# The end of a diffusion layer on one core: token lists by matmul, experts' rows gathered and stored by index, the gate applied on the experts' results, and the last residual sum on TensorE

## The reference, cut to what matters

```python
gates: top-1 group of 4, then top-2 of its 8 experts   # 32 experts, 640 * 2 = 1280 (token, expert) pairs
y_e   = down_e(silu(gate_e(h2)) * up_e(h2))             # D -> 256 -> D, for each chosen expert e
moe   = w_top1 * y_e1 + w_top2 * y_e2
x     = LN(ALPHA * x1 + gate2 * moe) * ln2_g + ln2_b    # gate2: one row of D for context, one for latent tokens
```

## Time and profile before

| | us |
|---|---|
| median of 3 runs (2627.85 to 2636.6) | 2629.16 |
| the profiled execution, its own time | 2629.61 |
| its span, first to last instruction | 2627.7 |
| `merge` | 1720.5 to 2087 |
| `route` | 2087 to 2254 |
| `experts` | 2254 to 2565 |
| `combine` | 2565 to 2627.7 |

### The profile page before, as it was taken

The page is one execution under the profiler, slowest core; times in us unless marked ns, Lnnn a source line. Parts: engine busy times, 40 slices in busy tenths (PEclk is TensorE's granted clock), DMA queues, the critical chain, the costliest instruction groups (busy, mean ns, idle before and its releaser), DMA issues. The chain is left out here.

```text
span 2627.7 us, 27002 instructions
## 1 busy us (share of the span) xinstructions
PE 2209.9 (84%) x9907; PEld 1374.1 (52%) x9907; DVE 1068.0 (41%) x1914; ACT 508.5 (19%) x1185; POOL 373.2 (14%) x379
## 2 busy tenths in 40 slices
PE   4789889899897989898898988889999795598980
PEld 2454555455544757667585776745555444343430
DVE  3574564665743454553535545410000056111116
ACT  0121211212202323323232332300000000111111
POOL 0041051230411011010201102000000000200005
PEclk9989989899898989899998989989999896799995
DMA  7011201101001010101101010043242295399973
GB/s 267 9 49 30 65 9 40 48 8 40 32 13 55 22 34 4 32 4 34 34 2 34 4 32 14 17 144 121 73 144 72 78 306 216 141 412 420 421 322 123
DMA packets 161406, 257.71 MB, mean 98 GB/s; under 512 B 11458, under 2 KB 127257, under 8 KB 147009
## 3 DMA queue, kind: packets, MB, share of 16 engines
q1 hardware_dynamic: 150905, 221.52, 24.0%
q10 hardware_dynamic: 5512, 18.56, 1.8%
q0 software_dynamic: 4928, 16.79, 1.7%
HBM read 229.26 MB, written 27.58 MB: 98 GB/s over the span
## 5 line engine op out<-in xcount | busy, mean ns | idle before, releaser
L642 PE MATMUL bank<-hT,shared 128*128 128x512 f32 x512 | 252.9, 629 | 13.3 <-DMA negm<-in_levels_dram 8.5
L1132 PE MATMUL bank<-hT,shared 128*128 128x512 f32 x384 | 175.4, 611 | 2.9 <-ACT spadded L1271 1.6
L1974 PE MATMUL bank<-ring,xgT 128*64 128x512 f32 (+1 forms) x416 | 151.6, 634 | 25.4 <-DMA ring<-in_w_exp_up_dram 13.0
L988 DVE TENSOR_TENSOR conv<-bank,negm 128x512 f32<-128x512 f32 x144 | 82.3, 599 | 184.4 <-PE bank L655 184.4
L642 PEld LDWEIGHTS bank<-hT,shared 128*128 128x128 f32 x512 | 94.7, 201 | 96.8 <-issue 88.1
L1212 PE MATMUL bank<-shared,hT 128*128 128x512 f32 x320 | 139.9, 592 | 0.0
L655 PE MATMUL bank<-D_,MT 128*128 128x128 f32 x960 | 125.4, 279 | 0.0
L1585 DVE SCALAR_TENSOR_TENSOR prod<-gth,bank 128x512 f32<-128x512 f32 x16 | 11.0, 687 | 272.7 <-PE bank L1559 272.7
L663 PE MATMUL bank<-DT,conv 128*128 128x128 f32 x960 | 121.6, 275 | 0.0
L1132 PEld LDWEIGHTS bank<-hT,shared 128*128 128x128 f32 x384 | 73.9, 197 | 89.7 <-issue 85.9
L1194 PEld LDWEIGHTS bank<-xT,M 128*128 128x128 f32 x640 | 88.4, 218 | 54.6 <-issue 41.3
(11 more groups left out here) (394 smaller groups left out, 3557.7 us busy)
## 6 DMA issues: line engine op xcount, KB each, us to landing
shared<-in_w_in_dram SPq DMA_DIRECT2D x58, 512.0 KB, 6.3
ring<-in_w_exp_gate_dram SPq DMA_DIRECT2D x26, 1024.0 KB, 18.1
ring<-in_w_exp_up_dram SPq DMA_DIRECT2D x26, 1024.0 KB, 20.4
ring<-in_w_exp_down_dram SPq DMA_DIRECT2D x26, 1024.0 KB, 15.4
aw<-in_w_ada_dram SPq DMA_DIRECT2D x8, 2048.0 KB, 7.5
yd<-ysb ACTq DMA_DIRECT2D x22, 512.0 KB, 8.3
aw<-in_w_ada_dram SPq DMA_DIRECT2D x8, 1024.0 KB, 21.5
shared<-in_w_in_dram SPq DMA_DIRECT2D x4, 2048.0 KB, 7.6
```

What stands on the lines that cost most here:

```text
L642: last = pe.matmul(bank[a][:, :], w4[:, n, k, :], hT[:, k, SEQ:T], start=(k == 0), stop=(k == KD - 1), skip_group_check=True)
L988: TT(out=X[:, u0:u0 + n, :], in0=bank[XB[g]][:, 0:n * P].rearrange("p (u n) -> p u n", n=P), in1=m, op=ALU.mult).then_inc(s["g_Xkept"], 1)
L1132: pe.matmul(bank[a][:, :], wn(n)[:, k, :], hT[:, k, SEQ:T], start=(k == 0), stop=(k == KD - 1))
L1974: last = pe.matmul(bank[2 + slot][at, :], xgT[:, slot, k, at], wgu[w][:, k, :, :], start=(k == 0), stop=(k == KD - 1))
```

## The change

- In `route` the token list no longer goes by way of memory. DVE makes for each of the ten blocks of 128 pairs a 128x128 matrix that marks the pair's place within its row of places (`at_place`) and a 128x22 matrix with the token number plus 1 in the column of its row (`of_row`). PE adds the ten products in one bank. A place that holds 0 is empty; its index becomes NOWHERE (2 to the power 20), beyond the bounds that the indirect transfers now get. `dest` holds for each place its own number, or a number out of bounds. DVE also waits once for the zeroed `lists` tail, as `zero` now lies in `h2`.
- The first two gathers of `xg` are issued in `route`. The scatters into `lists` (which only spill blocks still need) are issued in `experts` behind the fourth gather.
- The gather of a pass and its store to `yd` are bounded by index: rows of empty places are not moved. The store is an indirect transfer on POOL.
- All of `yd` (4032 rows of 4 KB, 16.5 MB) is now zeroed in one transfer that ACT issues at the start of `merge`; before, 4864 KB of it was zeroed in `route` by SP.
- DVE chooses the gate row for each place (`gsel`) and multiplies both halves of the expert's result by it; ACT no longer copies or stores results. `g2` is loaded at the start of `experts`.
- In `combine` PE forms ALPHA * x1 plus the two weighted result rows in PSUM, with diagonal matrices `keep` (ALPHA on the diagonal) and `weigh` (the tokens' weights on it). DVE takes its statistics from the banks, ACT norms from the banks, and DVE does `back` for all five tiles.

The new tiles are made over existing ones, save a few small ones. The diff, cut to its core:

```diff
+                act.wait_ge(zero_ready, 1)
+                act.dma_start(yd.rearrange("(p b) (c n) -> p (b c) n", p=SLOT, c=4),
+                              zero[0:SLOT, :].unsqueeze(1).broadcast_to([SLOT, NPLACE // SLOT * 4, D // 4])).then_inc(yz_out, 16)
...
-                sp.dma_start(lists.rearrange("(p n) a -> p (n a)", p=SLOT), zero[0:SLOT, 0:NPLACE // SLOT]).then_inc(z_out, 16)
-                sp.dma_start(yd[NP * P:NPLACE, :].rearrange("(p b) (c n) -> p (b c) n", p=SLOT, c=4), zero[0:SLOT, :].unsqueeze(1).broadcast_to([SLOT, NMORE * 4, D // 4])).then_inc(yz_out, 16)
+                sp.dma_start(lists[NP * P:NPLACE, :].rearrange("(p n) a -> p (n a)", p=SLOT), zero[0:SLOT, 0:NMORE]).then_inc(z_out, 16)
...
-                sp.wait_ge(scattered, 16 * 2 * NT)
-                sp.dma_start(rows_[:, :], lists[0:NP * P, :].rearrange("(e n) a -> e (n a)", e=NP)).then_inc(rows_in, 16)
...
-                pe.wait_ge(rows_in, 16)
-                pe.transpose(bank[4][:, 0:NP], rows_[:, :], C(C_ID)[0:NP, 0:NP]).then_inc(rows_turned, 1)
+                pe.wait_ge(placed, 2)
+                for a in range(2 * NT):
+                    last = pe.matmul(bank[4][:, 0:NP], at_place[:, a, :], of_row[:, a, :], start=(a == 0), stop=(a == 2 * NT - 1))
+                last.then_inc(listed, 1)
...
-                for t in range(NT):
-                    for n in range(2):
-                        pool.indirect_dma_start(out=lists, out_offset=bass.IndirectOffsetOnAxis(ap=slots[:, t, n:n + 1], axis=0),
-                                                in_=cols[:, S_TOK + t:S_TOK + t + 1], in_offset=None).then_inc(scattered, 16)
-                pool.wait_ge(scattered, 16 * 2 * NT)
...
+                for p in range(2):
+                    pool.wait_ge(taken, 1)
+                    pool.wait_ge(xg_blank, 1)
+                    pool.indirect_dma_start(out=xg[:, p, :], out_offset=None, in_=h2d,
+                                            in_offset=bass.IndirectOffsetOnAxis(ap=idx[:, LISTED[p]:LISTED[p] + 1], axis=0),
+                                            bounds_check=T - 1, oob_is_err=False).then_inc(got[p], 16)
...
+                    if t == 1:
+                        dve.wait_ge(z_out, 16)
...
+                flat = slotf[:, :, :, :].rearrange("p n t a -> p (n t a)")
+                dve.wait_ge(ends_in, 16)
+                st.link(TT(out=over[:, :, :], in0=flat.unsqueeze(2).broadcast_to([P, 2 * NT, NP]), in1=ends[:, 0:NP].unsqueeze(1).broadcast_to([P, 2 * NT, NP]), op=ALU.is_ge))
+                st.link(dve.tensor_reduce(out=rowf[:, :].unsqueeze(2), in_=over[:, :, :], axis=AX.X, op=ALU.add))
+                st.link(STT(out=inrow[:, :], in0=rowf[:, :], scalar=-float(P), in1=flat, op0=ALU.mult, op1=ALU.add))
+                TT(out=at_place, in0=ends[:, NP:NP + P].unsqueeze(1).broadcast_to([P, 2 * NT, P]),
+                   in1=inrow[:, :].unsqueeze(2).broadcast_to([P, 2 * NT, P]), op=ALU.is_equal).then_inc(placed, 1)
+                st.link(TT(out=of_row[:, :, :], in0=cols[:, S_E:S_E + NP].unsqueeze(1).broadcast_to([P, 2 * NT, NP]),
+                           in1=rowf[:, :].unsqueeze(2).broadcast_to([P, 2 * NT, NP]), op=ALU.is_equal))
+                tok = cols[:, S_TOK:S_TOK + NT].unsqueeze(2).broadcast_to([P, NT, NP])
+                for n in range(2):
+                    last = STT(out=of_row[:, n * NT:(n + 1) * NT, :], in0=tok, scalar=1.0, in1=of_row[:, n * NT:(n + 1) * NT, :], op0=ALU.add, op1=ALU.mult)
+                last.then_inc(placed, 1)
...
+                dve.wait_ge(listed, 1)
+                empty = spare[:, 0:NP]
+                st.link(TS(out=empty, in0=bank[4][:, 0:NP], scalar1=0.0, scalar2=float(NOWHERE), op0=ALU.is_equal, op1=ALU.mult))
+                STT(out=idx[:, :], in0=bank[4][:, 0:NP], scalar=-1.0, in1=empty, op0=ALU.add, op1=ALU.add).then_inc(taken, 1)
+                st.link(STT(out=empty, in0=ends[:, 0:NP], scalar=cols[:, S_TOK:S_TOK + 1], in1=empty, op0=ALU.add, op1=ALU.add))
+                st.link(TS(out=dest[:, :], in0=empty, scalar1=-float(P), scalar2=None, op0=ALU.add))
+                st.link(dve.tensor_copy(slots[:, :, :], slotf[:, :, :, 0].rearrange("p n t -> p t n")))
...
-                dve.wait_ge(rows_turned, 1)
-                st.link(dve.tensor_copy(idx[:, :], bank[4][:, 0:NP]))
...
+                for cond in range(2):
+                    sp.dma_start(g2[:, cond, :], rows(ada[cond, 5 * D:6 * D])).then_inc(g2_in, 16)
...
+                def store(p):
+                    pool.wait_ge(y_dve, 2 * p + 2)
+                    pool.indirect_dma_start(out=yd, out_offset=bass.IndirectOffsetOnAxis(ap=dest[:, LISTED[p]:LISTED[p] + 1], axis=0),
+                                            in_=ysb[:, p % 2, :], in_offset=None, bounds_check=NP * P - 1, oob_is_err=False).then_inc(y_out[p % 2], 16)
...
+                for p in range(2, NP + 4):
...
+                        pool.indirect_dma_start(out=xg[:, par, :], out_offset=None, in_=h2d,
+                                                in_offset=bass.IndirectOffsetOnAxis(ap=idx[:, LISTED[p]:LISTED[p] + 1], axis=0),
+                                                bounds_check=T - 1, oob_is_err=False).then_inc(got[par], 16)
+                    if p >= 4:
+                        store(p - 4)
+                    if p == 3:
+                        for t in range(NT):
+                            for n in range(2):
+                                pool.indirect_dma_start(out=lists, out_offset=bass.IndirectOffsetOnAxis(ap=slots[:, t, n:n + 1], axis=0),
+                                                        in_=cols[:, S_TOK + t:S_TOK + t + 1], in_offset=None).then_inc(scattered, 16)
+                pool.wait_ge(scattered, 16 * 2 * NT)
...
-                    act.wait_ge(dn_done, p + 1)
-                    if p >= 2:
-                        act.wait_ge(y_out[p % 2], p // 2 * 16)
-                    act.copy(ysb[:, p % 2, 512:D], bank[6][:, :]).then_inc(y_act, 1)
-                    act.wait_ge(y_act, p + 1)
-                    act.wait_ge(y_dve, p + 1)
-                    act.dma_start(yd[LISTED[p] * P:(LISTED[p] + 1) * P, :], ysb[:, p % 2, :]).then_inc(y_out[p % 2], 16)
...
+                    if p > 0:
+                        dve.wait_ge(y_dve, 2 * p)
+                    dve.scalar_tensor_tensor(out=gsel[:, :], in0=gdif[:, :], scalar=prompt[:, LISTED[p]:LISTED[p] + 1], in1=g2[:, 1, :],
+                                             op0=ALU.mult, op1=ALU.add).then_inc(gsel_ready, 1)
                     dve.wait_ge(dn_done, p + 1)
+                    dve.wait_ge(gsel_ready, p + 1)
                     if p >= 2:
                         dve.wait_ge(y_out[p % 2], p // 2 * 16)
-                    dve.tensor_copy(ysb[:, p % 2, 0:512], bank[5][:, :]).then_inc(y_dve, 1)
...
+                    for h in range(2):
+                        dve.tensor_tensor(out=ysb[:, p % 2, h * 512:(h + 1) * 512], in0=bank[5 + h][:, :], in1=gsel[:, h * 512:(h + 1) * 512], op=ALU.mult).then_inc(y_dve, 1)
...
+            @block.tensor
+            def _(pe):
+                at = lambda t, h: bank[2 * (t % 4) + h][:, :]
+                def residual(t):
+                    for h in range(2):
+                        pe.matmul(at(t, h), keep[:, :], x1[:, t, h * 512:(h + 1) * 512], start=True, stop=False)
+                pe.wait_ge(keep_ready, 1)
+                for t in range(4):
+                    residual(t)
+                pe.wait_ge(weigh_ready, 1)
+                for t in range(NT):
+                    if t == 4:
+                        pe.wait_ge(normed, 1)
+                        residual(t)
+                    pe.wait_ge(got[t], 32)
+                    for h in range(2):
+                        for n in range(2):
+                            last = pe.matmul(at(t, h), weigh[:, 2 * t + n, :], yg[:, t, n, h * 512:(h + 1) * 512], start=False, stop=(n == 1))
+                    last.then_inc(r_done, 1)
             @block.scalar
             def _(act):
                 for t in range(NT):
-                    act.wait_ge(got[t], 32)
-                    act.activation(yg[:, t, 0, :], yg[:, t, 0, :], ACT.Copy, scale=wts[:, t, 0:1]).then_inc(scaled, 1)
-                for t in range(NT):
                     act.wait_ge(nb_ready, t + 1)
-                    act.activation(yg[:, t, 1, :], x1[:, t, :], ACT.Identity, bias=nb[:, t:t + 1], scale=rs[:, t:t + 1]).then_inc(normed, 1)
-            def back(eng, t, weighed, at, out_ready):
-                a = yg[:, t, 1, :]
-                eng.wait_ge(normed, t + 1)
-                eng.tensor_tensor(out=a, in0=a, in1=lg[:, :], op=ALU.mult).then_inc(weighed, 1)
-                eng.wait_ge(weighed, at)
-                eng.tensor_tensor(out=x1[:, t, :], in0=a, in1=lb[:, :], op=ALU.add).then_inc(out_ready, 1)
+                    for h in range(2):
```

(32 more changed lines are left out.)

138 lines of the change are left out of this document (79 added, 59 removed).

## The result

The changed kernel takes 2589.28 us (median of 4 runs, 2587.12 to 2590.78) against 2631.37 us before on the same chip (2627.85 to 2636.6): ratio 0.9846, 95% interval 0.9831 to 0.9862, 42.1 us less. The forecast was 2589. The profiled execution took 2587.12, 1.9 more than its span.

The account below looks back on a forecast made before the run. Bytes bound `experts`, a chain without PE late `route`, DVE `combine`. From 2629.6 us, -2.7 - 11.6 - 10 + 1.3 - 19 + 2 = -40.0 gave 2589.6, against the median 2589; own range 2580 to 2596, with rivals 2570 to 2610.

Parts of the forecast that it names:

- a: `route`: zeroing of `yd` gone, so DVE's wait for a store behind it goes; -2.7 us.
- b: `route`: token list by matmul, PE starting 14.0 us after the places are known, against 25.6 before; -11.6 us.
- c: `experts`: fewer bytes moved; -10 us, taken in the lower half of -2.5 to -26.
- d: `experts`, last store: DVE does both result halves and POOL issues more slowly than ACT; +1.3 us.
- half the partitions means half the rate: `experts`: reason for taking 10 us, from zeroing by 64 partitions at 190 GB/s against 425 for full transfers.
- even saving: Rival on `experts`: all DMA engines lose alike, c at its upper end; 16 us less, 2573; chance 0.2.
- clean 0: Rival on `experts`: no fewer bytes where it counts, or skipped rows still cost a slot; 2597; chance 0.2.
- The estimate by the map of the Trainium skill: `experts`: partitions go to DMA engines in blocks of four; busiest loses 21 of 136 rows, c about 11 us.
- The prediction's own sign for c: Late passes of `experts`: a pair and a single fall from 27.6 to 26.5 us, above PE's 22.9.
- e: `combine`: PE forms the sums, DVE does `back` without POOL; end 38.5 us after first gather, before 58.3; -19 us.
- f: `merge`: zeroing 16.5 MB on ACT's queue delays the second slice; +2 us, between 0 and +12.

Follow-up runs that it names:

- e8: Changed kernel, but the two gate rows are loaded once more, into a tile nobody reads, in the full stretch of `experts`; 2594.31 us.
- e9: Changed kernel, but the last of the 22 stores to `yd` is a plain transfer on ACT's queue; 2586.86 us, ratio to the kernel before 0.9839.

## Why the prediction was right, step by step

The span shrank by 42.5 us. By the lengths: 1.4 lay ahead of the change's first effect (PE reached the second slice of `merge` at 1765.25, before at 1766.63, with no wait for weights), and is chance: in the other kernels whose second slice waits for nothing the same mark lies between 1764.45 and 1770.52.

*a, -2.7: right.* The places come 4.1 us earlier, 2.7 without that 1.4. From PE's second slice to the places it is 467.96 us before and 465.2 to 465.4 in all ten kernels with the change and zeros of 1 KB. DVE's wait for the store of `h2d` is in no row any more, and PE's waits for DVE's `h` in `route` fell from 12.5 to 9.8 us.

*b, -11.6: measured -10.2.* The steps were as costed: index at 8.4 us (8.6 said), `order` done at 12.9. Then the prediction took 0.8 us for the stage to turn; it took 2.5. The runs point to the gathers that were issued in the stage. From the end of `order` to PE's start it takes 4.6 us with all rows moved, 4.2 with clumped places, 2.5 in the changed kernel, 1.7 with spread places, and 0.7 with spread places and only the first gather in the stage. That fits a stage that turns only when the gathers issued in it have landed; where `order` ends last, the turn takes about the 0.8 us assumed.

*c, -10, and d, +1.3: measured together -9.4, -8.7 said.* The choice in the lower half held, and so did one of its reasons: the filled rows are a pass's first, and by assignment A the busiest DMA engine keeps 115 of its 136 rows. The other reason does not carry it. The 190 GB/s from 64 partitions were read as "half the partitions means half the rate", but the engines were 85% busy in that row, which eight of 16 can't be; zeros from the same 64 partitions, nearly alone, ran at 293 GB/s from 1760 to 1766 in the changed kernel and at 205 from 1766 to 1770. So that the size came out as 10 is partly luck. The even saving (2573) did not come, and the clean 0 (2597) did not either: the empty rows are 8.5 us. `g2` was not told apart (e8). With d at its 1.3, c is 10.7. The estimate by the map of the Trainium skill ("DMA: Bandwidth & Descriptors", section on the descriptor swizzle), about 11, is as near as the 10 that was taken, since the length moves by more than that on its own.

The prediction's own sign for c was the pace of the late passes, 27.6 us for a pair and a single falling to 26.5. By PE's transposes eight late passes took 109.5 us before (27.4 for two) and 105.4 or 107.7 in the changed kernel, by where one begins to count (26.4 or 26.9), and 100.1 or 101.2 with spread places: above PE's 22.9 in all three. (Its 1169 filled places are right, though the whole rows are not those of the twelve most loaded experts: the first five belong to experts 0 to 4 whatever their load, with 111 tokens in all.)

*d missed one thing:* from the last store to the first gather 8.1 us instead of 5.6. From PE's last matmul to the first gather it is 3.7 us more than before, not 1.3. The prediction counted DVE's second half and the longer issue, and nothing for the later start on POOL's queue nor for the store's way to memory; e9, with a plain store, is 3.2 us shorter there.

*e, -19: measured -21.4, and the forecast was better than that looks.* Same code in other executions takes up to 38.4, where 38.5 was said. What differs is when PE's clock comes back: the 16 records of ALPHA x1 take 8.6 us here and 9.1 to 10.2 in others (9.6 said), with a granted clock of 0.81 from 2544 to 2552 and 1.00 right after. A tile takes 4.9 us, 5.1 was said.

*f, +2: nothing, no stall.* The mechanism is the one assumed: each engine took as many pieces from the one queue as from the other. Its price was too high: 2308 couples in 10 us over 16 engines are 0.069 us each, where 0.086 was taken from zeros that ran alone from 64 partitions at 190 GB/s, the slowest stretch of such zeros with no other queue beside them (see c). 448 of them make 7.6 us less.

In sum -1.4 - 2.7 - 10.2 - 9.4 + 2.4 - 21.4 = -42.7, against 42.5 of the span. The right total owes something to luck: 1.4 of chance, 0.7 of c and d, 2 of f and 2.4 of e stand against 1.4 of b and the 2.4 missing in d. And the 2589 was 40.0 us below a kernel before at 2629.2; beside the changed kernel that one took 2631.4, so the time was met closer than the difference, 42.1.
